# Local attention with the values as weights: the output comes turned, the inverse softmax sums are turned too, and the rms factor moves to the residual sum

## What is computed

```python
def windowed_gqa(q, k, v, sink):            # 8 query heads of 64, 2 key/value heads, blocks of 128
    kw, vw = band(k), band(v)               # a block's own keys and those of its neighbours
    s = einsum('bnqhgd,bnkhd->bnhgqk', qb, kw) / sqrt(HEAD_DIM)
    s = where(mask, s, NEG)
    m = maximum(max(s), sink_l)
    p = exp(s - m)
    denom = sum(p) + exp(sink_l - m)
    o = einsum('bnhgqk,bnkhd->bnqhgd', p / denom, vw)

def rms_norm(x, g):
    return x * rsqrt(mean(square(x)) + RMS_EPS) * g

y_att = rms_norm(windowed_gqa(aq, ak, av, sink), att_g)
x = layer_norm(ALPHA * x + concatenate([y_att, y_ml]) @ w_out)
```

## Time and profile before

| | |
|---|---|
| median of 3 runs | 2225.08 us (2221.23 to 2226.53) |
| the profiled execution's own time | 2230.33 us |
| its span, first to last instruction | 2228.5 us |
| mean granted TensorE clock | 0.979 of full speed |
| busy: TensorE, VectorE, ScalarE, GpSimd | 2104.0, 1331.5, 991.3, 226.0 us |

### The profile page before, as it was taken

One profiled execution on the slowest core, in us unless ns is written; L12 is line 12 of the kernel. 1 busy time (PEld: TensorE's weight loads), 2 busy tenths in 40 slices (PEclk: granted clock), 3 DMA queues, 4 the chain that ended last, 5 costly groups with the idle time before them and its releaser, 6 DMA issues.

```text
span 2228.5 us, 31496 instructions
## 1 busy us (share of the span) xinstructions
PE 2104.0 (94%) x11392; PEld 1699.3 (76%) x11392; DVE 1331.5 (60%) x2057; ACT 991.3 (44%) x1616; POOL 226.0 (10%) x268
## 2 busy tenths in 40 slices
PE   7989989999999899999798999999999989999997
PEld 7779967888887577777577897778887767777773
DVE  4875487722454765656877647783235476666557
ACT  3554565232422455555245557533333235555552
POOL 0000023000000421001100001300000032100004
PEclk9999999999998999999999999999999999999998
DMA  4154112321102699999511112033120069999995
GB/s 153 57 198 147 39 76 96 105 85 57 57 29 98 252 368 371 386 382 349 189 53 38 39 45 89 20 133 114 57 76 20 32 230 389 375 379 371 377 372 202
DMA packets 78531, 384.85 MB, mean 173 GB/s; under 512 B 10472, under 2 KB 11864, under 8 KB 43608
## 3 DMA queue, kind: packets, MB, share of 16 engines
q1 hardware_dynamic: 55264, 327.31, 38.8%
q0 software_dynamic: 10096, 30.38, 3.9%
q10 hardware_dynamic: 13064, 25.75, 3.1%
HBM read 352.27 MB, written 46.07 MB: 179 GB/s over the span
## 4 chain that ended last, share of the span: by engine, by line
PE 71%; DVE 15%; ACT 8%; issue 3%; DMA 2%; POOL 1%; DVEq 0%; ACTq 0%; POOLq 0%; SPq 0%
PE bank L2197 29%; PE bank L2709 9%; PE bank L2683 8%; PE bank L2673 7%; PE bank L2410 5%; PE bank L2441 2%; ACT scratch L1055 2%; PE bank L2520 2%; DVE scratch L1595 2%; PE bank L2218 1%; DVE weight_slots_parts L1433 1%; PE bank L2649 1%; PE bank L2564 1%; PE bank L2580 1%; DVE small L1601 1%
## 5 line engine op out<-in xcount | busy, mean ns | idle before, releaser
L1903 DVE TENSOR_TENSOR weight_slots_parts<-weight_slots,mixer_region_parts 128x2048 fp32r<-128x2048 f32 x140 | 322.2, 2322 | 84.9 <-ACT mixer_region_parts L1257 84.8
L2197 PE MATMUL bank<-weight_slots_parts,x_transposed_parts 128*128 128x256 f32 (+1 forms) x1248 | 300.3, 335 | 8.6 <-DVE mixed L1555 5.7
L2197 PE MATMUL bank<-x_transposed_parts,weight_slots_parts 128*128 128x512 f32 (+1 forms) x1024 | 265.1, 346 | 8.3 <-DVE mixer_region L1547 5.1
L1257 ACT ACTIVATE mixer_region_parts<-weight_slots 128x2048 fp32r<-128x2048 f32 x140 | 261.1, 1910 | 23.5 <-ACT x_transposed L1332 18.1
L1433 DVE TENSOR_TENSOR weight_slots_parts<-weight_slots,weight_slots_parts 128x2048 fp32r<-128x2048 f32 x58 | 133.0, 2292 | 193.6 <-ACT weight_slots_parts L950 192.8
L2709 PE MATMUL bank<-weight_slots,x_transposed 128*128 128x512 f32 x560 | 247.4, 595 | 0.1
L2197 PEld LDWEIGHTS bank<-weight_slots_parts,x_transposed_parts 128*128 128x128 f32 x1248 | 211.6, 194 | 28.0 <-DVE mixed L1555 6.5
L2683 PE MATMUL bank<-mixer_region_parts,x_transposed_parts 128*128 128x256 f32 x1120 | 207.5, 283 | 1.0 <-DVE weight_slots_parts L1903 0.9
L2197 PEld LDWEIGHTS bank<-x_transposed_parts,weight_slots_parts 128*128 128x128 f32 x1024 | 181.6, 194 | 31.5 <-DVE mixer_region L1547 6.4
L2673 PE MATMUL bank<-mixer_region_parts,x_transposed_parts 128*128 128x512 f32 x560 | 191.8, 414 | 4.6 <-DVE x_transposed_parts L1908 4.6
L2709 PEld LDWEIGHTS bank<-weight_slots,x_transposed 128*128 128x128 f32 x560 | 104.0, 191 | 118.5 <-issue 103.0
(11 more groups left out here) (319 smaller groups left out, 3577.7 us busy)
## 6 DMA issues: line engine op xcount, KB each, us to landing
weight_slots<-in_w_gate SPq DMA_DIRECT2D x70, 1024.0 KB, 7.4
weight_slots<-in_w_up SPq DMA_DIRECT2D x70, 1024.0 KB, 7.1
weight_slots<-in_w_down SPq DMA_DIRECT2D x70, 1024.0 KB, 8.0
weight_slots<-in_w_in SPq DMA_DIRECT2D x20, 1024.0 KB, 5.1
slots_y<-x_transposed ACTq DMA_DIRECT2D x66, 256.0 KB
weight_slots<-in_wkv_mem SPq DMA_DIRECT2D x16, 1024.0 KB, 4.8
slots_y<-in_consts SPq DMA_DIRECT2D x6, 2304.0 KB, 16.8
weight_slots<-in_w_out SPq DMA_DIRECT2D x8, 1024.0 KB, 4.8
```

The costliest lines, as they stand in the source:

```text
L1257: nc.scalar.activation(hi, raw, ACT.Copy).then_inc(moe.high_ready, 1)
L1903: v.tensor_tensor(lo, raw, hi.bitcast(F32), ALU.subtract).then_inc(moe.low_ready, 1)
L2197: ins = pe.matmul(ps, lhs[i](k), rhs[j](k), start=k == 0 and a == 0, stop=k == KD - 1 and a == 2)
```

## The change

1. The product with the values is turned round. The values are the weights (128 rows, 64 columns) and the turned probabilities of two heads move (256 columns). The result has features in the partitions and tokens in the columns; the two key/value heads write partitions 0 to 63 and 64 to 127 of one bank.
2. The inverse sums must be turned too. VectorE's inverse now writes each of the 4 numbers 64 times (256 columns, `share_rows`), TensorE turns them in two transposes (tile `sr`, in banks 4 and 5), ScalarE copies them (`shares`) right after the item's exponentials, and VectorE multiplies them in at the eviction.
3. The six chunks need no turning afterwards: the 24 transposes of `yt` (first half) are gone. ScalarE makes the high parts from SBUF (`high_y`), VectorE the low parts (`low_y_attention`).
4. The rms factor is no longer applied to the chunks (the six L1573 are gone). The squares are summed over the feature groups by VectorE (`sum_squares`) and over partitions by TensorE (`sum_tokens`, tiles `rs`); ScalarE makes the factor after the last stream tile (`attention_rstd`), and it is multiplied in at the sum (`attention_half`). ALPHA is folded into it and applied at `add_half`.
5. The gains go into the weights `wo0` and `wo1`: four scaled copies on ScalarE and four operations on VectorE in place of one each. The rows of `w_out` are reordered on the host.

```diff
         if i:
+            add(("sr", i - 1), (4, 5))
             add(("pv", i - 1), (4, 5))
...
+    add(("rs", 0), (4, 5))
...
-                for c in YT_BEHIND[s] if g == 0 else ():
-                    add(("yt", c, 0), (4, 5, 6, 7))
+            if g == 0:
+                add(("rs", 1), (7,))
...
+                        elif name in ("wo0", "wo1"):
...
+                            for j in range(GRP - 1):
+                                nc.scalar.activation(hi[:, j, :], raw[:, j, :], ACT.Copy, scale=lane_gain[:, j:j + 1])
+                            nc.scalar.activation(hi[:, GRP - 1, :], raw[:, GRP - 1, :], ACT.Copy,
+                                                 scale=lane_gain[:, GRP - 1:GRP]).then_inc(w_hi, 1)
...
                     def square_of(c):
                         tile_drained(act, ("pv", 2 * c + 1))
...
-                        step(nc.scalar.activation(esc[:, :], y[:, c, 0:ATT], ACT.Square, accum_out=st[:, 20 + c:21 + c]))
+                        nc.scalar.activation(out, y_turned[:, c, 0:GRP, :], ACT.Square).then_inc(turned, 1)
+                        own(turned)
+
+                    def attention_rstd(part, c0, n):
+                        key = ("rs", part)
+                        tile_filled(act, key)
...
+                    def high_y(c):
+                        tile_filled(act, STREAM[-1])
+                        nc.scalar.activation(x_hi[:, 0:GRP, c * P:(c + 1) * P], y_turned[:, c, 0:GRP, :], ACT.Copy).then_inc(turned, 1)
+                        own(turned)
...
                             own(p_ready)
+                        if i:
+                            if i > 1:
+                                tile_drained(act, ("pv", i - 2))
+                            drain_copy(("sr", i - 1), shares, 2 * P)
 
                         if 7 <= i < 12:
                             square_of(i - 7)
-                        if i == 11:
-                            rstd(st[:, 20:25], st[:, 20:25], 5, 1.0 / ATT, eps_rms).then_inc(att_rs, 1)
-                            own(att_rs)
...
                                     for c in ((), (0, 1), (2, 3, 4), (5,))[sc]:
-                                        high_x(("yt", c, 0), c, 0)
+                                        high_y(c)
                         if g == 0:
                             stream_tile(STREAM[-1])
+                            attention_rstd(0, 0, NC - 1)
+                            attention_rstd(1, NC - 1, 1)
...
+                        elif name in ("wo0", "wo1"):
+                            lo, hi, raw = half_lo(name, GRP), half_hi(name, GRP).bitcast(F32), half_raw(name, GRP)
+                            for j in range(GRP):
+                                ins = v.scalar_tensor_tensor(out=lo[:, j, :], in0=raw[:, j, :], scalar=lane_gain[:, j:j + 1], in1=hi[:, j, :],
+                                                             op0=ALU.mult, op1=ALU.subtract)
+                            ins.then_inc(w_lo, 1)
...
+                    def sum_squares(c):
+                        dve.wait_ge(turned, len(TURNED) * now[0] + TURNED[("squares", c)] + 1)
+                        sq = qT[:, :, c * P:(c + 1) * P] if c < NC - 1 else esc[:, :].rearrange("p (j t) -> p j t", j=GRP)
+                        v.tensor_reduce(sums_at(c), sq.rearrange("p j t -> p t j"), AX.X, ALU.add).then_inc(att_parts, 1)
+                        own(att_parts)
...
                             dve.wait_ge(p_ready, 12 * l + i)
-                            ro = 110 + 4 * ((i - 1) % 2)
-                            step(v.tensor_tensor(st[:, ro:ro + 4], st[:, 8:12], st[:, 12:16], ALU.add))
-                            step(v.reciprocal(st[:, ro:ro + 4], st[:, ro:ro + 4]))
+                            step(v.tensor_tensor(st[:, 110:114], st[:, 8:12], st[:, 12:16], ALU.add))
+                            v.reciprocal(share_rows.rearrange("p (t d) -> p t d", t=GRP),
+                                         st[:, 110:114].unsqueeze(2).broadcast_to([P, GRP, HD])).then_inc(shares_ready, 1)
+                            own(shares_ready)
...
-                        if i == 12:
-                            dve.wait_ge(att_rs, 2 * l + 1)
-                            for c in range(NC - 1):
-                                attention_scaled(c)
                         if i:
                             c, jp = GROUP_ORDER[i - 1]
                             key = ("pv", i - 1)
                             tile_filled(dve, key)
...
+                            tile_drained(dve, ("sr", i - 1))
+                            v.tensor_tensor(y[:, c, 2 * P * jp:2 * P * (jp + 1)], bank_of(key)[:, 0:2 * P], shares, ALU.mult).then_inc(drain_sem(key), 1)
                             tile_drained(dve, key)
+                        if i >= 8:
+                            sum_squares(i - 8)
                         for t in w[1:]:
                             stream_tile(t)
...
+                    def attention_half(h, c):
...
+                        v.scalar_tensor_tensor(out=xh, in0=bank_of(key)[:, :], scalar=st[:, 20 + c:21 + c], in1=xh,
+                                               op0=ALU.mult, op1=ALU.add).then_inc(drain_sem(key), 1)
...
-                        v.tensor_tensor(xh, xh, bank_of(key)[:, :], ALU.add).then_inc(drain_sem(key), 1)
+                        v.scalar_tensor_tensor(out=xh, in0=xh, scalar=ALPHA, in1=bank_of(key)[:, :],
+                                               op0=ALU.mult, op1=ALU.add).then_inc(drain_sem(key), 1)
...
                                 spread_maxima(0)
+                            pe.wait_ge(shares_ready, 12 * l + i)
+                            ps = take(("sr", i - 1))
+                            for j in range(2):
+                                ins = pe.transpose(ps[:, j * P:(j + 1) * P], share_rows[:, j * P:(j + 1) * P], ident)
+                            done(ins, ("sr", i - 1))
...
-                            for t in range(GRP):
-                                n, _ = head_at(jp, t)
-                                for k in range(nb):
-                                    ins = pe.matmul(ps[:, t * HD:(t + 1) * HD], ptb[:, (t * nb + k) * P:(t * nb + k + 1) * P],
-                                                    kv[:, k0 + k, NKV * HD + n * HD:NKV * HD + (n + 1) * HD],
+                            for k in range(nb):
+                                for n in range(NKV):
+                                    out = ps[n * HD:(n + 1) * HD, 0:2 * P].rearrange("p (j q) -> p j q", j=2)
+                                    mine = ptb[:, 0:GRP * nb * P].rearrange("p (j n k q) -> p n k j q", j=2, n=NKV, k=nb)[:, n, k, :, :]
+                                    ins = pe.matmul(out, kv[:, k0 + k, NKV * HD + n * HD:NKV * HD + (n + 1) * HD], mine,
                                                     start=(k == 0), stop=(k == nb - 1))
                             done(ins, key)
...
+                    def sum_tokens(part, c0, n):
...
+                            pe.wait_ge(att_parts, 12 * l + c + 1)
+                            ins = pe.matmul(ps[:, c - c0:c - c0 + 1], sums_at(c), one, start=True, stop=True)
+                        done(ins, key)
+
+                    sum_tokens(0, 0, NC - 1)
...
-                                for c in YT_BEHIND[sc] if g == 0 else ():
-                                    pe.wait_ge(y_att, 6 * l + c + 1)
-                                    turn4(("yt", c, 0), lambda k: y[:, c, k * P:(k + 1) * P])
+                            if g == 0:
+                                sum_tokens(1, NC - 1, 1)
```

100 lines of the change are left out of this document (65 added, 35 removed).

## The result

The changed kernel takes 2281.68 us (median of 4 runs, 2274.63 to 2288.34) against 2224.74 us before (4 runs, 2221.23 to 2226.53; one more than stood ahead of the prediction). The ratio is 1.0257 with a 95% interval of 1.0219 to 1.0296: slower, as forecast, but by 57 us where 34 were forecast, and above the range (2237 to 2274). The profiled execution took 2277.47 us, its span is 2275.9 us; against the profiled execution before that is 47 us more.

What follows compares the result with a forecast made beforehand. It took a VectorE-ScalarE loop to set the pace, except TensorE in steps 7 and 8; 9.5 + 0 + 0.9 + 4.9 + 1.7 = 17.0 us a layer, 34 us for two, gave 2259 us (range 2237 to 2274).

Steps and rivals of the forecast that it cites:

- The mechanism named first: Inverse of 256 columns heading each VectorE step, before the mask steps: 1748 ns, 1.57 us more per item, 18.8 us a layer.
- the split of `wo1`: Groups 1 and 2: four-piece split, +0.5 and +0.7 us, hidden beside the early sums; 1.2 us a layer if uncovered.
- the sum of squares: VectorE, steps 8 to 12: reducing 512 columns takes 0.69 us, in front of a drain that TensorE may want.
- TensorE's work counts: Rival, chance 0.06: the loop's additions are all hidden and only TensorE's savings show, 2212 us.
- nothing changes: Rival, chance 0.06: the inverse takes 0.42 us and most small additions are hidden, 2225 us.
- the cheap inverse: Rival, chance 0.12: the inverse costs the same as any 256-column operation, 0.42 us; 6 us a layer, 2237 us.
- The rival of halves in turn: Rival, chance 0.14: the product's column halves don't run side by side; 3 us a layer more, 2265 us.
- The wait at the `sr` transposes: Sign: TensorE would wait for the inverse at the transposes of the inverse sums in steps 1, 2, 11 and 12.
- Steps 1 to 6: Loop-paced steps: inverse 1.57 and copy 0.4 us each, 11.8 us, less 2.3 absorbed at step 3; 9.5 us a layer.
- Steps 7 and 8: TensorE-paced steps: 0.16 us gained an item, value tiles drained 0.4 us later within the slack; sum 0.
- Steps 9 to 11: Chains ending in gate drains that TensorE awaits: +0.9 us at step 9, +4.9 us for steps 10 and 11.
- Step 12 and group 0: Inverse, output, token sums and rms factors before the first early sum, less VectorE's saved work: about 1.7 us later.

Runs made afterwards that it cites:

- the filled run: Changed kernel with TensorE's idle times in eight of the steps filled with 5 to 15 identity transposes each, which nobody reads: 2273.02 us, ratio 1.0228.
- The last filling: Changed kernel with 4-column inverse, two operations moved back and small tiles' banks changed (2243.93 us), plus identity transposes in TensorE's remaining gaps: 2244.97 us, ratio 1.0087.

## Why the prediction was right in sign and short in size

The mechanism named first, the wide inverse at the head of VectorE's step, is the right one and the largest part. The sum is short by 23 us because it had two terms at nothing, the lower granted clock behind TensorE's new waits and the split of `wo1`, and one too small, the sum of squares.

**What held.** The inverse: 1748 ns forecast, 1753 measured; alone in the kernel before it makes 41 us, taken back out of the changed kernel it gives 27 to 29, and the mechanism (head of VectorE's step, ahead of the mask steps) is shown by the same start of step 7 in both kernels. The product at 1.06 and 1.49 us: 1.08 and 1.52. The copy, 0.39: 0.384. The rivals that TensorE's work counts and that nothing changes are out, as is the cheap inverse. The rival of halves in turn is out twice: they overlap, and their order has no price. The wait at the `sr` transposes came in steps 1, 11 and 12, not in step 2.

**What failed**, in the order of the sum:

- *"Steps 1 to 6 ... sum 9.5 us"* is 11.5 us. The sum counted the waits that the inverse makes and took every later operation of TensorE at its old duration. TensorE stands 3.24 us in step 1, 1.72, 1.72 and 1.21 us in step 3 (1.87, 1.78 and 1.22 before the change) and 4.20 us in step 5, and in the 4 us behind these waits its clock is 0.50 to 0.57. The clock was in the earlier trace rows (0.93 and 0.97) and no term was made of it. That it costs time is shown in the kernel before (ratio 0.9969, 7.8 us by the medians). In the changed kernel the filled run says 6 to 9 us and its trace 7.0, and brings step 7 to 9.6 us late, the forecast's figure. The last filling, ill placed, gained nothing.
- *"Steps 7 and 8 ... Sum 0"* is 0.5 us: each takes 15.63 us for 15.38 before. TensorE does gain on the product, but its next stream tile then waits 0.37 us for ScalarE's copy of a value tile (L1026), which stands behind the new copy.
- *"The sum of squares reduces 512 columns, 0.69 us by the nearest reduce"*: 1.03 us. The nearest row reads 512 columns in order and leaves 2; the new one writes 128 and reads across four groups. Leaving it out took 4.3 us off layer 0 by the first early sum; the forecast had it at 0.7 in steps 9, 10 and 11 and none in step 12. Steps 9 to 11 together add 7.7 us where 5.8 were said, steps 7 and 8 included.
- *"Step 12 and group 0 ... +1.7 us"* is 4.1 us (23.3 less 19.2). The order was right (inverse, output, token sums); the token sums took 1.85 to 2.23 us, against 1.1, and the product before them 1.98 us against 1.08, all at 0.50 of the clock. With the gaps filled this step is 2.0 us.
- *"I let the second split (`wo1` ...) pass as hidden"*: this step is wrong outright. 17.0 forecast and 23.3 measured at the first early sum became 26.2 by the last one that waits, 2.9 us that stood at nothing. In the kernel before the pieces cost 5.9 us in layer 0 by themselves, of which 4.1 behind the first early sum; left out of the changed kernel they give 2.0. The prediction's price if uncovered, 1.2 us, was short because it took the low part at 4 x 0.75; in that place it takes 4.56 (kernel before) and 4.74 us (changed kernel). The high part, four copies of 0.71 us and not 0.60, adds 0.6.

**Readings that were off without harm.** The 1.02 us of L2353 in the earlier trace rows are eight transposes (x8, one record each), not four: two are worth 0.26 us and not 0.51, and `sr` takes 0.38. The 24 transposes that fall away were likewise priced at 6.1 us and were busy for 3.3. Neither moved the sum. Nor do the scores' 1.06 us by themselves show a drain: in the trace their records start in pairs, one of each half, 0.32, 0.22 and 0.22 us apart, and the last pair runs on for 0.38 us; whether the first, longer distance is a drain is not shown.

**The balance.** Put alone into the kernel before, the inverse makes 41 us and the pieces 10: 51 of 57. Taken out of the changed kernel, the inverse gives 27 to 29 us and the pieces 4 to 6. So the parts do not simply add: what one costs depends on which waits the others leave. Taking the inverse back, moving two operations and changing banks brings the loss from 57 to 14.5 us by the medians (17 by the ratio). How the pieces, the sums and the clock share that rest is not shown.

## What to carry to other kernels

Price an instruction that is put at the head of a dependent loop by every round of the loop, and add what the lower clock makes of the busy engine's work behind each new wait. Broadcast before a cheap operation, not through an expensive one: the inverse of 4 columns read 64 times by TensorE did the same for 0.18 us of VectorE and 0.3 us more of TensorE. A part's price found by adding it alone and by taking it out alone can differ by a third and more; measure both. Before cutting one VectorE operation into pieces, look at what GpSimd does beside it.

## What the runs showed of the hardware

- An inverse over 256 columns takes 1753 ns, on the line through 4, 16 and 64 columns (6.2 ns a column); over 64 partitions it takes 1749.
- Transposes that nobody reads, 44 a layer in gaps of 1.2 to 1.9 us, made the kernel before 0.3% faster, and the granted clock stayed at 1.00 where it had been 0.55 to 0.60. The Trainium skill, TensorE: Matmul & The Clock Gate, section What's actually happening, has the clock set by how busy TensorE has recently been, at 1.2 or 2.4 GHz; the windows agree (0.50 and 1.00, and values between them elsewhere).
- A wait does not by itself bring the low clock: 3.24 us before 99.39 us is followed by 0.50, 3.31 us before 257.60 us by 1.00.
- Two column halves work side by side in this precision: records start in pairs 7 ns apart, four matmuls take 1.08 us and six 1.52.
- A sum over four groups of 128 columns takes 1025 ns, against 692 for 512 columns in order from PSUM.
- A VectorE piece of 512 columns takes 0.75 us alone and up to 1.77 beside a GpSimd operation on SBUF; one of 2048 columns takes 2.29 us beside it, and GpSimd's operation 2.51.
